# A decoder's sliding-window attention on one core: both blocks' probabilities added into one tile before one transpose a head

## What is computed

```python
# each of 2 layers: T = 512 tokens, 16 query heads of 64, 2 key/value heads, blocks of 128
kb, vb = band(k), band(v)           # for each block of 128: previous block and current block, 256 keys
s = einsum('bnqkgd,bnskd->bnkgqs', qb, kb) * scale
rel = qi + BLOCK - sj               # qi: 0..127 in the block, sj: 0..255 in the band
mask = (rel >= 0) & (rel < 128) & (kpos >= 0)
s = where(mask, s, -inf)
m = maximum(max(s), sink)
p = exp(s - m); p = p / (sum(p) + exp(sink - m))
o = einsum('bnkgqs,bnskd->bnqkgd', p, vb)
merged = sigmoid(ga) * o + sigmoid(gb) * conv_branch
```

## Time and profile before

| | us |
|---|---|
| runs shown (3) | 2247.91, 2248.34, 2249.16 |
| median | 2248.34 |
| span of the profiled execution, first to last instruction | 2246.4 |
| PE busy in it | 2224.9 |
| DVE busy | 1245.1 |
| ACT busy | 885.6 |
| POOL busy | 280.7 |

### The profile page before, as it was taken

How to read it: one execution, slowest core, us unless ns; L and a number is a source line. 1 busy time by engine, 2 the same in 40 slices (tenths; PEclk the granted TensorE clock), 3 DMA queues, 4 the chain that set the end, 5 groups by cost and what they waited for, 6 DMA issues and landing times.

```text
span 2246.4 us, 29245 instructions
## 1 busy us (share of the span) xinstructions
PE 2224.9 (99%) x11388; PEld 1821.7 (81%) x11388; DVE 1245.1 (55%) x1836; ACT 885.6 (39%) x1363; POOL 280.7 (12%) x273
## 2 busy tenths in 40 slices
PE   9999999999999999999999999999999999999999
PEld 7877888898888888886778888888887668888887
DVE  6467656445444225999664444333889664544422
ACT  5545454354333225234744333222323753433321
POOL 3000032011000001014331000001003442000000
PEclk9999999999999999999999999999999999999999
DMA  6221033122222231321122222222221112322222
GB/s 223 100 76 57 20 121 126 55 72 99 103 102 93 94 113 69 113 75 57 56 77 81 107 93 93 100 106 105 104 84 57 39 66 85 113 102 104 94 101 86
DMA packets 30484, 203.19 MB, mean 90 GB/s; under 512 B 3504, under 2 KB 4144, under 8 KB 6704
## 3 DMA queue, kind: packets, MB, share of 16 engines
q1 hardware_dynamic: 29088, 197.34, 24.4%
q10 hardware_dynamic: 1296, 4.46, 0.5%
HBM read 199.69 MB, written 2.10 MB: 90 GB/s over the span
## 4 chain that ended last, share of the span: by engine, by line
PE 93%; DVE 3%; POOL 1%; ACT 1%; issue 1%; DMA 0%; ACTq 0%; DVEq 0%; POOLq 0%
PE bank L415 26%; PE bank L417 26%; PE bank L416 26%; PE bank L2110 1%; PE bank L1002 1%; PE bank L2120 1%; PE bank L2133 1%; PE bank L973 1%; PE bank L2028 1%; POOL acc L324 1%; PE bank L990 1%; PE bank L2010 1%; PE bank L1593 1%; PE bank L1570 1%; PE bank L515 1%
## 5 line engine op out<-in xcount | busy, mean ns | idle before, releaser
L415 PE MATMUL bank<-x_hi,w_hi 128*128 128x512 f32 (+1 forms) x2032 | 789.9, 389 | 5.9 <-DVE x_lo L1766 2.3
L417 PE MATMUL bank<-x_hi,w_lo 128*128 128x512 f32 (+1 forms) x2032 | 775.0, 381 | 0.0
L416 PE MATMUL bank<-x_lo,w_hi 128*128 128x512 f32 (+1 forms) x2032 | 774.1, 381 | 0.0
L301 DVE TENSOR_TENSOR w_lo<-w_raw,w_hi 128x2048 fp32r<-128x2048 f32 x167 | 386.2, 2313 | 412.3 <-ACT w_hi L297 412.3
L297 ACT ACTIVATE w_hi<-w_raw 128x2048 fp32r<-128x2048 f32 x167 | 319.7, 1916 | 585.8 <-PE bank L417 583.9
L415 PEld LDWEIGHTS bank<-x_hi,w_hi 128*128 128x128 f32 x2032 | 382.1, 188 | 83.6 <-issue 6.8
L417 PEld LDWEIGHTS bank<-x_hi,w_lo 128*128 128x128 f32 x2032 | 381.9, 188 | 74.9
L416 PEld LDWEIGHTS bank<-x_lo,w_hi 128*128 128x128 f32 x2032 | 382.4, 188 | 72.7 <-issue 2.9
L415 PE MATMUL bank<-f_hi,w_hi 128*128 128x512 f32 (+1 forms) x572 | 213.3, 373 | 0.0
L416 PE MATMUL bank<-f_lo,w_hi 128*128 128x512 f32 (+1 forms) x572 | 213.2, 373 | 0.0
L417 PE MATMUL bank<-f_hi,w_lo 128*128 128x512 f32 (+1 forms) x572 | 213.2, 373 | 0.0
(11 more groups left out here) (355 smaller groups left out, 2637.2 us busy)
## 6 DMA issues: line engine op xcount, KB each, us to landing
w_raw<-w_d SPq DMA_DIRECT2D x184, 1024.0 KB, 4.8
out_d<-h SPq DMA_DIRECT2D x8, 256.0 KB, 6.6
h<-x_d ACTq DMA_DIRECT2D x3, 512.0 KB, 9.2
tab<-rope_d ACTq DMA_DIRECT2D x2, 640.0 KB, 3.9
memT<-mem_d ACTq DMA_DIRECT2D x1, 1024.0 KB, 4.8
w_raw<-w_d SPq DMA_DIRECT2D x2, 256.0 KB, 4.1
h<-x_d ACTq DMA_DIRECT2D x2, 256.0 KB, 5.8
w_raw<-w_d SPq DMA_DIRECT2D x1, 512.0 KB, 6.6
```

The source lines that it names most:

```text
L301: dve.tensor_tensor(w_lo[:, u.slot, :], w_raw[:, u.slot, :], w_hi[:, u.slot, :], ALU.subtract).then_inc(lo_ready, 1)
L415: pe.matmul(dst, wh[:, k, cols], hi[:, kx_, at:at + width], start=start, stop=False)
L416: pe.matmul(dst, wh[:, k, cols], lo[:, kx_, at:at + width], start=False, stop=False)
L417: return pe.matmul(dst, wl[:, k, cols], hi[:, kx_, at:at + width], start=False, stop=stop)
```

## The change

For the 24 jobs of a layer that have a previous block (`banded`):

- POOL first adds the previous block's probabilities to the current block's, in one tile of 128x128 a head (`band_sums`), and then scales that tile alone.
- PE transposes this one tile a head: two transposes a job, into the first half of bank 4. ACT copies the half (`lprobT[:, :, 0:2]`).
- DVE (`cut`) multiplies the same half of bank 4 by `neg_cur`, which is -1 where the key belongs to the current block and 0 elsewhere, into `lprobT[:, :, 2:4]`. It stands in step t for job t-3, behind `gated(t-4)`; it waits for ACT's copy of that job and, before job 0, for `neg_cur`.
- PE's values are the transposed sum times the previous block's values, plus the cut part times `lvd`, the previous block's values less the current one's: four products as before. The second pair waits for `lvd` and for the cut.
- `turn(j)` now also waits for the cut of job j-1.
- `lvd` (128x384) lies in `cos_q` and is made once a layer by POOL, before the first sink column. `neg_cur` lies in `perm_q` and is made once a layer by DVE in step 2.

In the first block's mixer, semaphores are merged (`kcm_ready`, `kcm_dup` into `kc_rope`; `cmp_sum` into `cmp_weight`); the waits stay where they were.

```diff
+        lvd, neg_cur = cos_q[:, 0:3 * P], perm_q
...
             def turn(j):
-                first = 1 if block_of(j) == 0 else 0
                 pe.wait_ge(A["scaled"], L * LJ + j + 1)
                 if j:
                     pe.wait_ge(A["turned_copied"], L * LJ + j)
+                    pe.wait_ge(band_cut, L * BANDS + min(j, BANDS))
                 for e in range(2):
-                    for c in range(first, 2):
-                        mm = pe.transpose(bank[:, 4, (2 * e + c) * P:(2 * e + c + 1) * P], lprob[:, prob_at(j), e, c * P:(c + 1) * P], ident[:, :])
+                    mm = pe.transpose(bank[:, 4, e * P:(e + 1) * P], lprob[:, prob_at(j), e, P:2 * P], ident[:, :])
                 mm.then_inc(A["turned"], 1)
...
             def values(j):
                 i, g = block_of(j), j % 8 // 4
-                first = 1 if i == 0 else 0
...
-                for c in range(first, 2):
+                for e in range(2):
+                    mm = pe.matmul(bank[HD * e:HD * e + HD, 6, 0:P], lv[:, max(i - 1, 0), g * HD:(g + 1) * HD],
+                                   lprobT[:, j % 2, e, :], start=True, stop=not banded(j))
+                if banded(j):
+                    pe.wait_ge(band_sums, L * (BANDS + 1) + 1)
+                    pe.wait_ge(band_cut, L * BANDS + j + 1)
                     for e in range(2):
-                        mm = pe.matmul(bank[HD * e:HD * e + HD, 6, 0:P], lv[:, i - 1 + c, g * HD:(g + 1) * HD],
-                                       lprobT[:, j % 2, 2 * e + c, :], start=(c == first), stop=(c == 1))
+                        mm = pe.matmul(bank[HD * e:HD * e + HD, 6, 0:P], lvd[:, (i - 1) * P + g * HD:(i - 1) * P + (g + 1) * HD],
+                                       lprobT[:, j % 2, 2 + e, :], start=False, stop=True)
                 mm.then_inc(A["pv"], 1)
...
-                act.activation(lprobT[:, j % 2, :, :].rearrange("p (e c) t -> p e c t", e=2)[:, :, first:, :],
-                               bank[:, 4, :].rearrange("p (e c t) -> p e c t", e=2, c=2)[:, :, first:, :], ACT.Copy)\
+                act.activation(lprobT[:, j % 2, 0:2, :].rearrange("p e t -> p (e t)"), bank[:, 4, 0:2 * P], ACT.Copy)\
                    .then_inc(A["turned_copied"], 1)
...
+            def cut(j):
+                dve.wait_ge(A["turned_copied"], L * LJ + j + 1)
+                if j == 0:
+                    dve.wait_ge(band_ready, L + 1)
+                if j >= 2:
+                    dve.wait_ge(A["pv"], L * LJ + j - 1)
+                dve.tensor_tensor(lprobT[:, j % 2, 2:4, :], bank[:, 4, 0:2 * P].rearrange("p (e c) -> p e c", e=2),
+                                  neg_cur[:, :].unsqueeze(1).to_broadcast([P, 2, P]), ALU.mult).then_inc(band_cut, 1)
...
                 if 0 <= t - LAG_V < LJ:
                     gated(t - LAG_V)
+                if 0 <= t - LAG_T < BANDS:
+                    cut(t - LAG_T)
...
                 if t == 2:
                     roped(4)
+                    dve.scalar_tensor_tensor(out=neg_cur[:, :], in0=mask_b[:, P:2 * P], scalar=-1.0, in1=ident[:, :],
+                                             op0=ALU.max, op1=ALU.subtract).then_inc(band_ready, 1)
...
             def scaled(L, j):
-                c0 = P if block_of(j) == 0 else 0
-                row = lprob[:, prob_at(j), :, c0:2 * P]
+                prev, row = lprob[:, prob_at(j), :, 0:P], lprob[:, prob_at(j), :, P:2 * P]
                 pool.wait_ge(A["exp"], (L * LJ + j + 1) * 2)
+                if banded(j):
+                    pool.tensor_tensor(row, row, prev, ALU.add).then_inc(band_sums, 1)
+                    pool.wait_ge(band_sums, L * (BANDS + 1) + j + 2)
                 pool.wait_ge(A["rec"], L * LJ + j + 1)
-                pool.tensor_tensor(row, row, asm(j, 12).unsqueeze(2).to_broadcast([P, 2, 2 * P - c0]), ALU.mult).then_inc(A["scaled"], 1)
+                pool.tensor_tensor(row, row, asm(j, 12).unsqueeze(2).to_broadcast([P, 2, P]), ALU.mult).then_inc(A["scaled"], 1)
...
                     if j == 0:
+                        pool.wait_ge(q_cos, L * 9 + 9)
+                        pool.wait_ge(l_v, L * 4 + 4)
+                        pool.tensor_tensor(lvd.rearrange("p (b c) -> p b c", b=3), lv[:, 0:3, :], lv[:, 1:4, :], ALU.subtract).then_inc(band_sums, 1)
```

More of the change, by code:

```diff
@@ L682, in build @@
             "xf_ready", "xc_hi_ready", "xc_lo_ready", "xf_pe", "hid_ready", "hid_turned", "hc_ready"))
-        kc_step, vc_done, kc_rope, kcm_ready, kcm_dup, vblk_ready = (
-            sem(n) for n in ("kc_step", "vc_done", "kc_rope", "kcm_ready", "kcm_dup", "vblk_ready"))
+        kc_step, vc_done, kc_rope, vblk_ready = (
+            sem(n) for n in ("kc_step", "vc_done", "kc_rope", "vblk_ready"))
+        KC_PLACED, KC_DOUBLED = 4, 5
         conv_step, csq_ready, cstat_done, cstd_ready, cinv_ready, crow_done, cn_ready, mix_hi, mix_lo = (sem(n) for n in (
             "conv_step", "csq_ready", "cstat_done", "cstd_ready", "cinv_ready", "crow_done", "cn_ready", "mix_hi", "mix_lo"))
-        c_sub, c_sum, c_w = sem("cmp_sub"), sem("cmp_sum"), sem("cmp_weight")
+        c_sub, c_w = sem("cmp_sub"), sem("cmp_weight")
         j_s, j_max, j_neg, j_exp, j_rec, j_w, j_t, j_pta, j_ptd, j_pv, j_o = (sem("job_" + n) for n in (
@@ L924, in c_scores @@
                 if i == 0:
-                    pe.wait_ge(kcm_dup, 1)
+                    pe.wait_ge(kc_rope, KC_DOUBLED)
                     pe.wait_ge(rope_done, 6)
@@ L1176, in mixer1_act @@
             split_hi(act, Unit(10))
-            act.wait_ge(kcm_ready, 1)
-            act.activation(kcm[HD:P, :, :], kcm[0:HD, :, :], ACT.Copy).then_inc(kcm_dup, 1)
+            act.wait_ge(kc_rope, KC_PLACED)
+            act.activation(kcm[HD:P, :, :], kcm[0:HD, :, :], ACT.Copy).then_inc(kc_rope, 1)
             for n in (11, 12):
@@ L1388, in mixer1_dve @@
             dve.wait_ge(const_ready, 3)
-            dve.tensor_copy(kcm[0:HD, :, 0:NCMP], kc2[:, :, :]).then_inc(kcm_ready, 1)
+            dve.tensor_copy(kcm[0:HD, :, 0:NCMP], kc2[:, :, :]).then_inc(kc_rope, 1)
             gated_out(2)
@@ L1413, in c_weights @@
                 dve.wait_ge(j_exp, i + 1)
-                dve.tensor_reduce(csm(i, 16), e_c[:, i % 2, :].rearrange("p (h c) -> p h c", c=32), AX, ALU.add).then_inc(c_sum, 1)
-                dve.wait_ge(c_sum, i + 1)
+                dve.tensor_reduce(csm(i, 16), e_c[:, i % 2, :].rearrange("p (h c) -> p h c", c=32), AX, ALU.add).then_inc(c_w, 1)
+                dve.wait_ge(c_w, 4 * i + 1)
                 dve.tensor_scalar(csm(i, 16), csm(i, 16), 1e-30, None, ALU.max).then_inc(c_w, 1)
-                dve.wait_ge(c_w, 3 * i + 1)
+                dve.wait_ge(c_w, 4 * i + 2)
                 dve.reciprocal(csm(i, 16), csm(i, 16)).then_inc(c_w, 1)
-                dve.wait_ge(c_w, 3 * i + 2)
+                dve.wait_ge(c_w, 4 * i + 3)
                 g0 = gate[:, i, :].rearrange("p (m e b) -> p e m b", e=2, b=3)[:, :, :, 0]
@@ L1425, in c_combine @@
                 dve.wait_ge(j_pv, i + 1)
-                dve.wait_ge(c_w, 3 * i + 3)
+                dve.wait_ge(c_w, 4 * i + 4)
                 dve.tensor_tensor(o_all[:, i, :].rearrange("p (m e d) -> p e m d", e=2, d=HD),
@@ L1940, in build @@
         sink_in = sem("a_sink_in")
+        band_ready, band_sums, band_cut = sem("a_band_ready"), sem("a_band_sums"), sem("a_band_cut")
+        BANDS = 24
         LJ = QB * 8
@@ L1984, in block_of, with banded @@
             return (j // 8 + 1) % QB
+        def banded(j):
+            return block_of(j) > 0
         def query_factor(j, e=None):
```

## The result

The changed kernel takes 2255.67 us (median of 7 runs, 2253.03 to 2257.16) against 2248.54 us before (median of 7): ratio 1.0032, 95% interval 1.0022 to 1.0041. It is slower by 7.1 us (by the interval 4.9 to 9.2), so the loss is clear of the noise; forecast were 5.4. The 2248.34 us given ahead of the prediction are the median of three of these seven runs. The profiled execution has a span of 2254.7 us, 8.3 more than before.

What follows compares the result with a forecast made beforehand. PE was taken as the bound, busy 2224.9 of 2246.4 us. Per layer, head 1.8, 19 jobs 0.6 and late-DVE steps 0.3 make 2.7 us; twice that, +5.4 on 2248.34, gives 2253.7 us, range 2245 to 2261.

Steps and rivals of the forecast that it cites:

- the head: First steps of each attention, where DVE has no slack: PE 1.8 us late per layer.
- A saved transpose pair is 0.22 us: PE, 48 jobs: two of four transposes go, 0.22 us a job, 10.5 us in all as ceiling.
- The cut takes 0.42 us and its hand-over 0.14: DVE's new 128x256 product takes 0.42 us; PE's transposes start 0.14 us after it ends.
- The ordinary job: Steady step: 0.22 us saved, 0.25 us stall before the transposes, so +0.03 us a job.
- 19 more jobs at 0.03: Jobs of a layer after the head, each taken as an ordinary one: 0.6 us a layer.
- The taps lose 1.64 us: Head: POOL's subtraction and two additions, less shorter scaling, delay DVE's taps and PE's column sums of cy by 1.64 us.
- turn(2) 2.2 us late, turn(3) 2.4: Head: transposes of job 2 come 2.2 us late; PE about 2.4 us late at job 3, 2.2 after its saved transposes.
- The wait at the sums of squares swallows 0.26 us: Head: PE's earlier 0.26 us wait for POOL's sums of squares is swallowed by its lateness.
- Rival 1: Head: POOL's additions hardly touch the taps; head +0.4 to +0.6 us, kernel 2250.7 us; chance 0.32.
- Rival 2: Steady steps: the cut hides and PE keeps its gain; 2241 to 2245 us, said 2242; chance 0.13.
- Rival 3: Middle steps: DVE becomes the bound there too; +7 us on top, 2261 us; chance 0.13.

Runs made afterwards that it cites:

- e1: The changed kernel with the cut placed ahead of the gate in DVE's order: 2246.69 us, ratio 0.9988 to the kernel before.
- e8: The kernel of e1 with the new form only for blocks 2 and 3 (jobs 8 to 23): 2240.96 us, ratio 0.9967.
- e6: The kernel before plus DVE's cut into an unused tile, awaited by the next transposes, all four transposes kept: 2263.97 us, ratio 1.0064.
- e9: The kernel before plus only POOL's subtraction of the values (128x384), written to an unused tile: 2249.63 us, ratio 1.0006.
- e2: The changed kernel with PE's four chunks of step 5 ahead of that step's transposes: 2255.43 us, ratio 1.0028.
- e5: The kernel before plus POOL's subtraction and additions, written to an unused tile, scaling unchanged: 2254.65 us, ratio 1.0025.
- e3: The changed kernel with the edits of both e1 and e2: 2246.83 us, ratio 0.9991.
- e7: The kernel of e1 with the sums of squares and ACT's root in step 8 instead of 7: 2254.3 us, ratio 1.0024.
- e4: The kernel before with PE's step 5 chunks ahead of that step's transposes: 2249.7 us, ratio 1.0002.

## Why the prediction was right, and where its terms were not

The sign, the mechanism and nearly the size held: 2253.7 forecast, 2255.67 measured, inside the range. By layer the trace has 3.8 and 3.7 us where the sum had 2.7. That the head came as near as it did (2.6 us at job 5's transposes, 1.8 in the sum) is in part luck: the taps were put 0.9 us too high, and 1.4 us of half clock stood in no term.

- *A saved transpose pair is 0.22 us.* Right: 0.20 to 0.22 a job where nothing waits (e1, e8).
- *The cut takes 0.42 us and its hand-over 0.14.* Right: 416 ns, and 0.14 at 1084.52. The transposes start 0.81 us behind the values, as written. The ordinary job came to +0.03: from job 5 to job 19 the first layer loses 0.38 us, 0.03 a job. e6 shows the stall without the saving: 0.23 us a job.
- *19 more jobs at 0.03.* Wrong for the last four. The scores of steps 24 to 27 are block 0's, half as long (128 columns), so 0.21 us less stands between the values and the transposes. The step that failed is the statement that the transposes start 0.56 us after the values, taken from one step for all. From job 19 to job 24 the first layer loses 0.86 us; the sum had the 0.03 a job there, and 0.3 us a layer for steps where DVE is late for other reasons. It could have been read. The order of time of the kernel before has, just ahead of the 1129.20 of the earlier trace rows:

```profile
1128.19 0.66 PE L2133 MATMUL bank<-lprobT,lv 128*64 128x128 f32 x8
```

  The values end at 1128.85, and the transposes start 0.35 us later.
- *The taps lose 1.64 us.* Too much: 0.77. The subtraction costs 0.72 (e9; 0.83 said), the first addition 0.47 (0.62 said), the shorter scaling gives back 0.45 (0.43 said). The second addition, 0.62 in the sum, started at 1044.27 inside the last tap, which kept its 0.74 us: here it was the addition that waited (1.25 us). Its own length was also off: POOL's addition is 0.73 us where undisturbed, with two full tiles as inputs; I had taken the scaling's 0.615 for it.
- *turn(2) 2.2 us late, turn(3) 2.4.* The first was 1.6 us late, and the chain to it as described: gate at DVE's pace, cut behind it, 0.14. Then came what I had not: half clock behind the pause, 1.4 us net of the saved transposes' 0.22 from job 2's transposes to job 1's values, so that turn(3) was 3.2 us late.
- *The wait at the sums of squares swallows 0.26 us.* It swallowed 0.3 in the changed kernel, where PE was later than POOL. With PE less late, the wait at the same place is 0.6 to 1.2 us (e1, e2, e5) instead of 0.26. I had looked at POOL's additions only for what they do to DVE's taps, not for what stands behind them in POOL's own queue.
- *Rival 1* is refuted by the taps of 0.94 and 0.85 us on average instead of 0.70. (Its own sum is 0.1 to 0.3 us a layer short: a head of 0.4 to 0.6 us and 0.9 for the rest make 1.3 to 1.5 a layer, 2251 us.) *Rival 2* is refuted by the 0.81. *Rival 3*: DVE is not the bound in the middle; gates start 0.05 us behind the values in all but four jobs a layer (0, 4, 15 and 31), and job 31's 0.44 us stand in the kernel before too.

The lock. Three taps of 2.11 us took 2.83 beside a POOL subtraction that itself took 1.43, where 128x256 takes 0.73 and 128x512 1.09 us undisturbed. The Trainium skill, "SBUF — State Buffer", section "Who interferes with whom", has one engine wait for the whole instruction of the other; the rows agree, in that the loss falls on single instructions and not on a rate: in the trace of after, of the three taps beside the subtraction one took 1.50 us and the other two their 0.74; of the three beside the first addition one took 1.22.

Left open: what decides whether the clock falls. Every half-clock stretch in the attentions stood behind, or began in, a pause of PE, but the length of the pause does not tell which. Before the transposes the clock fell behind 1.95 us (changed kernel, both layers), 2.0 (e3, both) and 1.81 (e7, first layer); it stayed full behind 1.82 (e1, both layers; e7, second) and behind 2.16 and 2.11 (e2). At the sums of squares it fell behind 0.60 us (e2), 0.83 (e6), 0.71 (e4, second layer), 1.17 (e1, first) and 1.16 (e5, second), and stayed full behind the same 0.71 (e4, first), 1.16 (e1, second) and 1.17 (e5, first). That the pause brings the half clock is thus argued from where it stands, and not shown. A stretch costs 1.4 us in e5 and 1.6 in the changed kernel, with the saved 0.22 put back, and the two layers of e1 differ by one.

## What to carry to other kernels

- A new reader of a buffer holds up the next writer of it. Its place in its own engine's queue can be worth more than its length: here the same 0.42 us instruction, 48 times, costs some 9 us when it stands behind an instruction that waits for PE's values, and no stall when it stands ahead of it.
- A form that saves in the steady state can be left out where the engines that pay for it are full. Two thirds of the jobs in the new form were worth more than all of them.
- Filling a pause pays only if what caused it isn't late at the next place too; look two waits ahead before moving work into it.

## What the runs showed of the hardware that was not expected

- The granted clock fell to half (1.2 GHz of 2.4) for 3.4 us in the head of an attention, and products started 0.43 us apart instead of 0.23; in the changed kernel that made 1.6 us a layer, 1.4 net of a saved pair of transposes. In e7's first layer a stretch of 6.8 us began in a wait of 2.4 us. Pauses of the same length had it in one layer or run and not in another (1.82 and 2.16 us without, 0.60 us with).
- The taps and POOL stopped each other both ways: one tap took 1.50 us beside the subtraction, and the addition at 1044.27 took 1.25 us instead of 0.73 beside a tap.
- A wait that is one of several on an instruction took 0.14 us from the releaser's end to PE's next start (cut to transposes, copy to transposes), as the prediction had it; the tap to the column sums took 0.05.
- Where three semaphores are awaited, the trace's name for the releaser was wrong in some of these waits: "POOL" for what e1 shows to be DVE's cut.
